# Four edits to a one-layer bidirectional mixer and expert kernel: scan order, values as one 512-column unit, fewer states, a stacked gate product

## The reference

```python
# mLSTM heads (keys and values of 128): states per chunk, both directions
c_new = a_old * c_st + a_new * (sum_l e_l v_l k_l^T)     # the same for the vector n
h = (S v + a * (q C_prev)) / max(|den|, exp(-m))
# gated linear attention heads (keys of 64, values of 128), per direction d
la = log_sigmoid(a_lr[:, 16 d:16 d + 16] @ w_a2[d] + b_a[d]) / 16      # low-rank gate, rank 16
S_t = diag(exp(la_t)) S_{t-1} + k_t v_t^T;   o_t = q_t S_t
```

## Time and profile before

| | |
|---|---|
| median of 3 runs | 1364.94 us (1364.13 to 1365.88) |
| profiled execution | 1364.38 us, span 1362.7 us |
| granted TensorE clock, mean | 0.978 |
| value stage | 196.5 to 257.5 us |
| first scan | 257.5 to 333.3 us |
| o0 to the end of the query unit | 333.3 to 445.4 us |
| second scan | 559.7 to 629.2 us |
| TensorE, VectorE, ScalarE, GpSimd busy | 94%, 70%, 57%, 9% of the span |

### The profile page before, as it was taken

One profiled execution on the slowest core, in us unless ns is written; L12 is line 12 of the kernel. 1 busy time (PEld: TensorE's weight loads), 2 busy tenths in 40 slices (PEclk: granted clock), 3 DMA queues, 4 the chain that ended last, 5 costly groups with the idle time before them and its releaser, 6 DMA issues.

```text
span 1362.7 us, 19538 instructions
## 1 busy us (share of the span) xinstructions
PE 1278.2 (94%) x7427; PEld 1119.3 (82%) x7427; DVE 953.1 (70%) x1114; ACT 773.2 (57%) x918; POOL 119.2 (9%) x127
## 2 busy tenths in 40 slices
PE   5899999899999999989999399999999999999994
PEld 4888799898987999867888388888888888888883
DVE  5757420278655772476545878888888888888887
ACT  6643320375213644574334257777777777777785
POOL 1100000010000000013000020111111111111034
PEclk9999979999999999999999699999999999999997
DMA  9851151143445321304213879999999999999995
GB/s 369 271 120 34 62 158 44 39 137 121 155 186 185 124 81 76 140 1 170 81 75 140 322 267 367 388 406 397 397 397 395 397 394 397 391 402 392 400 318 207
DMA packets 78686, 320.45 MB, mean 235 GB/s; under 512 B 5544, under 2 KB 32200, under 8 KB 48856
## 3 DMA queue, kind: packets, MB, share of 16 engines
q1 hardware_dynamic: 71360, 291.18, 54.4%
q0 software_dynamic: 7264, 28.40, 8.3%
HBM read 292.20 MB, written 35.75 MB: 241 GB/s over the span
## 4 chain that ended last, share of the span: by engine, by line
PE 80%; DVE 10%; ACT 5%; DMA 3%; issue 2%; SPq 0%; POOLq 0%; DVEq 0%; ACTq 0%
PE psum L2538 36%; PE psum L2192 7%; PE psum L2474 6%; PE psum L2250 5%; PE psum L2251 5%; PE psum L2252 5%; PE psum L2278 1%; DMA ada_raw<-w_ada_units 1%; PE psum L2286 1%; PE psum L2287 1%; PE psum L2266 1%; PE psum L2093 1%; PE psum L2561 1%; ACT g_ps L1124 1%; PE psum L2555 1%
## 5 line engine op out<-in xcount | busy, mean ns | idle before, releaser
L1955 DVE TENSOR_TENSOR e_lo<-e_raw,e_hi 128x2048 fp32r<-128x2048 f32 x192 | 432.8, 2287 | 43.1 <-ACT e_hi L1274 43.0
L1274 ACT ACTIVATE e_hi<-e_raw 128x2048 fp32r<-128x2048 f32 x192 | 365.9, 1916 | 83.3 <-PE psum L2538 82.1
L2538 PE MATMUL psum<-e_hi,xt_hi 128*128 128x512 f32 x496 | 153.3, 390 | 0.1
L2538 PE MATMUL psum<-e_lo,xt_hi 128*128 128x512 f32 x496 | 152.9, 389 | 0.0
L2538 PE MATMUL psum<-e_hi,xt_lo 128*128 128x512 f32 x496 | 152.8, 389 | 0.0
L2250 PE MATMUL psum<-w_hi,h_hi 128*128 128x256 f32 x512 | 147.1, 287 | 0.5 <-issue 0.5
L2251 PE MATMUL psum<-w_hi,h_lo 128*128 128x256 f32 x512 | 145.8, 285 | 0.0
L2252 PE MATMUL psum<-w_lo,h_hi 128*128 128x256 f32 x512 | 145.8, 285 | 0.0
L2538 PEld LDWEIGHTS psum<-e_hi,xt_lo 128*128 128x128 f32 x496 | 93.1, 188 | 19.6
L2538 PEld LDWEIGHTS psum<-e_lo,xt_hi 128*128 128x128 f32 x496 | 93.1, 188 | 19.5
L2538 PEld LDWEIGHTS psum<-e_hi,xt_hi 128*128 128x128 f32 x496 | 92.8, 188 | 19.8 <-DVE xt_lo L1959 0.5
(11 more groups left out here) (414 smaller groups left out, 2330.3 us busy)
## 6 DMA issues: line engine op xcount, KB each, us to landing
...
```

The costliest lines, as they stand in the source:

```text
L1274: act.activation(e_hi[u % EH][:], e_raw[u][:], ACT.Copy).then_inc(e_hi_ok, 1)
L1955: dve.tensor_tensor(e_lo[u][:], e_raw[u][:], e_hi[u % EH][:], ALU.subtract).then_inc(e_lo_ok, 1)
L2538: m = pe.matmul(o[:, BANK * b:BANK * (b + 1)], x[:, k, :], w[:, D * j + BANK * b:D * j + BANK * (b + 1)], start=a, stop=z)
```

## The change

Four edits at once.

1. **Values as one unit.** v1 is loaded into a buffer of its own right behind v0 and split right behind it; the two halves' `hi` and `lo` lie so that one access of 2 x 256 columns covers both. TensorE runs 10 tiles of 24 products of 512 columns, one bank each; each is evacuated by one instruction. Row loads for the context's third and fourth `bc` buffers wait for all ten tiles.
2. **First scan.** Steps 18 and 19 do no transposes, key scaling, state products or state update (N_STEPS = 18). split_lo(o0) moves in front of the wait for the last numerators.
3. **Gate product.** The 32 gate rows of a direction, their `hi` and their `lo` are stacked on 96 partitions (zx), the weights likewise (zw), so that one fp32r product of 96 rows gives the sum of three. ScalarE makes the `hi` parts between the sigmoids, VectorE the `lo` parts between columns 11 and 12.
4. **Second scan.** On ScalarE wo_hi_part goes in front of gla_carry; on VectorE wo_lo_part works on the part of the step before (steps 2 to 9); GpSimd's square waits until VectorE has made g_kx three steps on, its product until g_qz three steps on.

```diff
+        V1 = AT["in", "v1"]
+        v1_raw = at("v1_raw", AT_RING + 24 * KB, [P, KC, UW])
+        vv_hi = at("vv_hi", AT_RING + 16 * KB, [P, 4, KC, UW], F32R)[:, 0:4:3, :, :]
+        vv_lo = at("vv_lo", AT_RING + 8 * KB, [P, 3, KC, UW], F32R)[:, 0:3:2, :, :]
...
+        zx = [at(f"zx{d}", AT_OUT + (36 + 5 * d) * KB, [P, ALL], F32R) for d in range(2)]
+        zw = at("zw", AT_OUT + 46 * KB, [P, 2 * GK_W], F32R)
+        zw_hi = at("zw_hi", AT_OUT + 48 * KB, [P, 2 * GK_W], F32R)
...
+        N_STEPS = 2 * TA - 2
...
             def load_unit(n):
-                if n >= 10 and n - 2 != O0:
+                if n == V1:
+                    sp.wait_ge(raw_full[0], 48)
+                elif n >= 10 and n - 2 != O0:
                     wait_used(sp, n - 2)
-                sp.dma_start(raw[n % 2][:], unit_src(*STREAM[n])).then_inc(raw_full[n % 2], 16)
+                sp.dma_start(raw_of(n)[:], unit_src(*STREAM[n])).then_inc(raw_full[n % 2], 16)
...
             load_bc(1, *scan_chunk(1))
-            sp.wait_ge(tok_mm, 5)
+            sp.wait_ge(tok_mm, 10)
             load_bc(2, 0, 1)
-            sp.wait_ge(tok_mm, 10)
             load_bc(3, 1, 0)
...
             for l in range(TL, 2 * TL):
                 t = second_visit(l)
                 pool.wait_ge(og_done, l + 1)
+                pool.wait_ge(kx_ready, 16 + min(l + 4, 2 * TL))
                 if l >= TL + 2:
                     pool.wait_ge(sq_read, l - TL - 1)
                 pool.tensor_tensor(g_sq[l % 2][:], og(t), og(t), ALU.mult).then_inc(gla_sq, 1)
+                pool.wait_ge(gx_ready, min(l + 4, 2 * TL))
                 v = og(t).rearrange("p (u n) -> p u n", u=2)
                 pool.tensor_tensor(v, v, silu_r(t), ALU.mult).then_inc(fin_done, 1)
...
             conv_first(6, 0, 0, False)
             conv_first(7, 0, 1, False)
             split_hi(13)
+            split_hi(14)
             conv_silu(6, 0, 0)
             conv_silu(7, 0, 1)
             conv_first(8, 0, 2, False)
             conv_first(9, 0, 3, False)
-            split_hi(14)
             conv_silu(8, 0, 2)
             conv_silu(9, 0, 3)
             act.wait_ge(stat_ready, 1)
-            for u in range(2):
-                for j in range(5):
-                    p = 5 * u + j
-                    if p % 2 == 0:
-                        act.wait_ge(tok_mm, p + 1)
-                        for r in range(2):
-                            i = act.activation(v_ext[:, 2 * j + r, 2 * u:2 * u + 2, 0:HD], tokv(p, r), ACT.Copy)
-                        i.then_inc(tok_act, 1)
+            for p in range(0, TA, 2):
+                act.wait_ge(tok_mm, p + 1)
+                act.activation(v_ext[:, p, :, 0:HD], tokv(p), ACT.Copy).then_inc(tok_act, 1)
...
             def ml_front(t, l, d, c):
-                act.wait_ge(kt_mm, t + 1)
-                at_least(act, kv_mm, t - 1)
-                for h in range(NH):
-                    i = act.activation(ml_kh[d][:, h, :], kt_ps[d][:, h, :], ACT.Copy,
-                                       scale=cst[:, 1, ds(c, 1), NH * d + h])
-                i.then_inc(kh_ready, 1)
+                if t < N_STEPS:
+                    act.wait_ge(kt_mm, t + 1)
+                    at_least(act, kv_mm, t - 1)
+                    for h in range(NH):
+                        i = act.activation(ml_kh[d][:, h, :], kt_ps[d][:, h, :], ACT.Copy,
+                                           scale=cst[:, 1, ds(c, 1), NH * d + h])
+                    i.then_inc(kh_ready, 1)
...
             o_gates(0)
             split_hi(17)
+            for d in range(2):
+                q = slice(32 * d, 32 * (d + 1))
+                act.activation(zx[d][q, :], gate_rows[q, :], ACT.Copy)
+            act.activation(zw_hi[64:96, :], col("w_gla2")[64:96, :], ACT.Copy).then_inc(z_hi_ok, 1)
             o_gates(1)
+            for d in range(2):
+                q = slice(32 * d, 32 * (d + 1))
+                act.activation(zx[d][64:96, :], gate_rows[q, :], ACT.Copy)
+            act.activation(zw[0:64, :], col("w_gla2")[0:64, :], ACT.Copy).then_inc(z_hi_ok, 1)
...
                     gla_exps(l + 2)
+                if 1 <= l < 9:
+                    wo_hi_part(l - 1)
                 if 1 <= l <= N_STATE:
                     gla_carry(l - 1)
-                if 1 <= l < 9:
-                    wo_hi_part(l - 1)
...
             split_lo(13)
+            split_lo(14)
             conv_taps(8, 0, 2)
             conv_taps(9, 0, 3)
 
             dve.wait_ge(stat_mm, 1)
             dve.tensor_copy(cst[:].rearrange("p q c s -> p (q c s)"), psum[:, 7 * BANK:7 * BANK + 3 * TA * 2 * NH]).then_inc(stat_ready, 1)
-            split_lo(14)
             dve.memset(v_ext[:, :, :, HD:HD + 1], 1.0).then_inc(ones_set, 1)
-            for u in range(2):
-                for j in range(5):
-                    p = 5 * u + j
-                    if p % 2 == 1:
-                        dve.wait_ge(tok_mm, p + 1)
-                        for r in range(2):
-                            i = dve.tensor_copy(v_ext[:, 2 * j + r, 2 * u:2 * u + 2, 0:HD], tokv(p, r))
-                        i.then_inc(tok_dve, 1)
+            for p in range(1, TA, 2):
+                dve.wait_ge(tok_mm, p + 1)
+                dve.tensor_copy(v_ext[:, p, :, 0:HD], tokv(p)).then_inc(tok_dve, 1)
...
+            def ml_back(t, l, d, c):
+                if t < N_STEPS:
+                    ml_state(t, l, d)
                 if l is None:
                     return
+                if l == 2 * TL - 1:
+                    split_lo(O0)
                 dve.wait_ge(num_mm, l + 1)
...
             scan_steps(dve, ml_front, ml_back)
-            split_lo(O0)
...
-            ada_columns(10, 11, 12)
+            ada_columns(10, 11)
+            dve.wait_ge(z_hi_ok, Z_HI + 1)
+            for d in range(2):
+                q = slice(32 * d, 32 * (d + 1))
+                dve.tensor_tensor(zx[d][32 * (1 - d):32 * (2 - d), :], gate_rows[q, :], zx[d][q, :], ALU.subtract)
+            dve.tensor_tensor(zw[64:96, :], col("w_gla2")[64:96, :], zw_hi[64:96, :], ALU.subtract).then_inc(z_lo_ok, 1)
+            ada_columns(12)
...
                     gla_scores(l + 1)
-                if 1 <= l < 9:
-                    wo_lo_part(l - 1)
+                if 2 <= l < 10:
+                    wo_lo_part(l - 2)
...
-            tok_unit("v0", 13, h_hi, h_lo, 0)
-            tok_unit("v1", 14, h_hi, h_lo, 0)
+            unit_ready(V1)
+            for p in range(TA):
+                if p >= TOK_BANKS:
+                    pair_out(pe, p - TOK_BANKS)
+                o = psum[:, BANK * (p % TOK_BANKS):BANK * (p % TOK_BANKS + 1)]
+                c = slice(P * p, P * (p + 1))
+                for k in range(KC):
+                    pe.matmul(o, h_hi[:, k, c], vv_hi[:, :, k, :], start=k == 0, stop=False)
+                    pe.matmul(o, h_lo[:, k, c], vv_hi[:, :, k, :], start=False, stop=False)
+                    last = pe.matmul(o, h_hi[:, k, c], vv_lo[:, :, k, :], start=False, stop=k == KC - 1)
+                last.then_inc(tok_mm, 1)
...
+                if t >= N_STEPS:
+                    return
                 at_least(pe, kh_ready, t - 1)
...
-                pe.wait_ge(kh_ready, t + 1)
-                at_least(pe, c_done, t)
                 vc = lambda h: v_ext[:, ds(c, 1), h, :]
-                for h in range(NH):
-                    i = pe.matmul(kv_ps[:, h // 2, h % 2, :], ml_kh[d][:, h, :], vc(h), start=True, stop=True)
-                i.then_inc(kv_mm, 1)
+                if t < N_STEPS:
+                    pe.wait_ge(kh_ready, t + 1)
+                    at_least(pe, c_done, t)
+                    for h in range(NH):
+                        i = pe.matmul(kv_ps[:, h // 2, h % 2, :], ml_kh[d][:, h, :], vc(h), start=True, stop=True)
+                    i.then_inc(kv_mm, 1)
+                else:
+                    pe.wait_ge(c_done, t - 1)
...
+                if i == 0:
+                    pe.wait_ge(z_hi_ok, Z_HI + 2)
+                    pe.wait_ge(z_lo_ok, Z_LO + 1)
+                w = lambda dp: zw[0:96, P * dp:P * (dp + 1)]
                 if i < 8:
                     q = CTX + BANK * (i % 2)
-                    pe.matmul(z_ps(i), w(i // 2), gate_rows[:, q:q + BANK], start=True, stop=True).then_inc(z_mm, 1)
+                    pe.matmul(z_ps(i), w(i // 2), zx[i // 4][0:96, q:q + BANK], start=True, stop=True).then_inc(z_mm, 1)
                 else:
                     for j in range(2):
-                        x = pe.matmul(z_ps(i)[:, CTX * j:CTX * (j + 1)], w(2 * (i - 8) + j), gate_rows[:, 0:CTX], start=True, stop=True)
+                        x = pe.matmul(z_ps(i)[:, CTX * j:CTX * (j + 1)], w(2 * (i - 8) + j), zx[i - 8][0:96, 0:CTX], start=True, stop=True)
                     x.then_inc(z_mm, 1)
```

30 lines of the change are left out of this document (19 added, 11 removed).

## The result

| | before | changed |
|---|---|---|
| median of the first runs | 1364.54 us (1363.11 to 1365.88) | 1341.81 us (1341.10 to 1349.21) |
| all executions in this study | 40: median 1363.2, mean 1363.4, 1359.5 to 1369.7 | 14: median 1342.2, mean 1343.3, 1339.6 to 1349.2 |

The median of the first runs is that of four executions; a fifth of the changed kernel took 1343.04. The direction was right and the gain was forecast too small.

The account below looks back on a forecast made before the run. TensorE, busy 94% of the span, was taken as the bound. Terms 3.05 + 2.4 + 6.3 + 4.9 + 1.2 = 17.85 us off the profiled 1364.38 gave 1346.5, 1347.1 as median; range 1344.3 to 1351.5.

Parts of the forecast that it names:

- Values: Value stage: 240 products of 512 columns for 480 of 256 save 3.05 us; bounds 0 to 3.2.
- Rival E: Value products: pitch is columns plus a trifle, so the values give only 0.6 us; 1349.5 us, chance 0.04.
- Last states: End of first scan and o stage: 4.1 us less one half-clock spell of 1.7 gives 2.4; bounds 0.7 to 4.1.
- rival A: End of first scan: no spell of half clock in the new waits; 1345.4 us, chance 0.13.
- Gate product: Gate stage: one-pass pieces at 0.23 us instead of 0.86 save 6.3 us on TensorE; bounds 0 and 6.5.
- Second scan: First-half steps at 3.93 us instead of 4.59 save 4.9; g_kx without GpSimd beside it in the second half saves 1.2.
- C: Second scan keeps another loop, step near 4.35 us, first-half gain only 2; 1350.0 us, chance 0.13.
- D: Gate product saves only half, as TensorE meets late columns or evacuations; 1350.2 us, chance 0.08.
- G: Reordered scan keeps its waits and the gate stack stays multi-pass; 1359.5 us, chance 0.02.
- B: End of first scan: half-clock spells in both new waits; 1348.8 us, chance 0.13.
- part 4: Second scan, first half, eight steps with output-weight splits: gain 4.9 us; bounds 6.3 (TensorE alone) and 1.
- F: Slower: TensorE's clock stays low after the first scan's new waits, deciding from about 18 us at 1.2 GHz; chance 0.01.

Follow-up runs that it names:

- spread_filled: Changed kernel with the little gate-row products spread behind the last two query tiles' slices, plus unread products in TensorE's waits at the first scan's end and behind the query tile: 1338.49 us.
- quiet_undo_values: spread_filled with the values as two units of 256 columns again: 1341.11 us.
- first trace: The profiled execution of the unaltered changed kernel, slowest of its set: 1349.21 us, span 1347.5.
- undo_values: Changed kernel with the values as before, two units of 256 columns, second load behind the last query tile: 1348.21 us.
- undo_gate: Changed kernel with the gate product in fp32 over 128 rows, as before: 1350.01 us.
- undo_scan1: Changed kernel with all twenty states of the first scan and unit o0's split behind the last output, as before: 1347.81 us.
- quiet_undo_scan1: spread_filled with all twenty first-scan states and o0's split behind the last output, without the unread products in the first scan: 1342.16 us.
- third trace: Changed kernel run again without edit, traced once more: median 1341.92 us, span of the trace 1340.0.
- the second: Changed kernel run again without edit, for another trace: median 1344.91 us, span of the trace 1345.4.

## Why the forecast was right and where it failed

- **Values: right.** 3.05 forecast, 3.0 to 3.2 at equal spells, 3.24 with none. Start to start, the 240 products of 512 columns in spread_filled are 0.2267 us apart and the 480 of 256 in quiet_undo_values 0.1200: the pitches of the earlier trace rows held. Rival E, which gave 0.6, is out. (The Trainium skill's formula for a single product in TensorE: Matmul & The Clock Gate, section Back-to-back issue gap, would make the two cost nearly alike, an estimated 0.6 us apart; the stage windows differ by 3.24 us.) The second load and the zero fill cost nothing that shows.
- **Last states: the step that failed.** "This trace drops to half clock after idles of 1.05 and 0.79 close together ... So I charge one spell at half clock, 1.7 us, and take 2.4 us." The waits came as worked out, 1.39 and 1.92 us in the first trace, but a spell behind them came in only three of the nine traces that have this part and no filler there (330.0 in the first trace, and undo_values and undo_gate). Where it stays away and the old order has its own spell behind the wait for o_lo, the gain is the gross 4.1: 0.14 in the scan (74.57 us for undo_scan1's 74.71) and 3.9 in the o stage. So rival A, 1345.4, was the likeliest case and stood at 0.13. The 1.7 us that the sum credits for the old order's spell is not certain either: three of the four traces of that order have it, quiet_undo_scan1 has not, and there the gain is 2.39. That this is the forecast's 2.4 is luck, since it is another sum (neither spell, instead of both). Over the traces, 2.4 + 1.7 x (3/4 - 3/9) gives about 3.1 us as an estimate of the average gain.
- **The same mistake at a larger size.** The forecast also carried the other spells of its one trace over, as things the change leaves alone: "The first 22 or so products run at the half clock in any case", and the spell at the scan's start. In the third trace the half clock at the values' start lasts 6.8 us instead of 13.7, which is worth 3.3 us, and the one at the scan's start is absent, which is worth 1.0 (scan 75.74 us before, 74.71 in undo_scan1, which has the same twenty states and no spell there). I took one trace's falls of the clock for what the program does; they are what it does in some executions.
- **Gate product: right.** 6.3 forecast, 6.32 to 6.33 in each pair of traces; a piece takes 0.23 us, as its price of the earlier trace rows had it for 128 rows; nothing in the stage waits for a column or an evacuation.
- **Second scan: right.** 4.9 + 1.2 = 6.1 forecast, 6.1 to 6.4 measured to the end. The starts of the scores in the first half are 3.87 us apart (561.92 to 573.53, three steps) where 3.93 was forecast. GpSimd's waits give their 1.2 in the scan (1.3 measured) and 0.7 to 0.9 in all. The last wo_lo, which moved beside GpSimd's square, took 1.23 us for 0.74 in the trace. (The estimate of 1 us from the Trainium skill's SBUF — State Buffer, section SBUF: two separate sides, was twice too large for it; the square had begun 0.36 us before it, at 590.46, and took 1.04.)
- **Rivals.** C, D, E and G are out by the stages above; B, spells in both waits, is in no trace. The range's floor was said to be A with part 4 at its bound, which gives 1344.0 (1345.4 less 6.3 - 4.9), not 1344.3; the measured time lies below both. F asked for 18 us of extra work at 1.2 GHz; the longest new spells are 3.4 to 6.8 us, and no run of the changed kernel comes near the one before.

**The rest of the miss.** On the average, 40 executions of the kernel before have a mean of 1363.4 and 14 of the changed one 1343.3: 20.1 us, for the 17.85 of the sum. Of the 2.25 between them the estimate above explains 0.7 (3.1 for 2.4). The rest is not attributed; it is no larger than the differences between sets (the kernel before's medians lie between 1361.46 and 1364.54). The forecast time was higher by another 1.5 us because its base, a median of three at 1364.94, lay that far above the mean of the forty.

The median shown first, 1341.81, is lower still. Four of its five executions were probably of the kind of the third trace (execution 1341.75, clock 0.979 as theirs); that is inferred from their times and mean clocks alone, for those four have no trace. The third trace is 22.6 us shorter than the profiled one before, 4.8 more than the sum. By stages: 2.65 of that in the scan and the o stage (5.05 for 2.4: the spell charged and the one at the scan's start), 3.3 in the shorter spell at the values' start, and 1.2 lost again, because this trace reaches the little products later (186.51 for 185.32 us). Gate stage and second scan give 0.1.

**The wait at 142.** The first trace idles 3.9 us for a key tile, the second 1.7 and the third 1.1, and the traces show why. First and third:

```profile
87.92 1.92 ACT L871 ACTIVATE w_hi<-raw 128x2048 fp32r<-128x2048 f32 x1 [4.54 <-DMA raw<-w_in_units]
...
142.44 1.19 PE L2223 MATMUL psum<-h_hi,w_hi 128*128 128x512 f32 x2 [3.89 <-DVE kT L1536]
```
```profile
88.37 1.92 ACT L871 ACTIVATE w_hi<-raw 128x2048 fp32r<-128x2048 f32 x1 [1.73 <-DMA raw<-w_in_units]
...
142.91 0.70 PE L2223 MATMUL psum<-h_hi,w_hi 128*128 128x512 f32 x2 [1.10 <-DVE kT L1536]
```

ScalarE's split of that unit waits for its landing. From the split, ScalarE and VectorE take 54.5 us to the tile in every one of the eighteen traces, and TensorE takes 56.5 us from the stage's first product (82.02 and 85.27 us here) to the wait; the load is issued 1.6 us before that product. What is left to vary is the load's time from issue to landing: 7.5 us in the first trace (80.40 to 87.9), 5.3 in the second, 4.7 in the third (83.64 to 88.3), and less 3.6 these are the three waits. The third trace began the stage 3.3 us later than the first and reached the tile only 0.5 later. A spell at 141 to 144 us stands in seven of the eight traces with the longer of these waits (1.98 to 4.01 us; the eighth is the kernel before, 2.30) and in none of the ten others (1.08 to 1.78), and the three traces with a spell at 330 are among the seven.

**What stays open.** What makes the landing of that load take 4.7 us or 7.5; what decides whether the clock falls at a wait that some traces pass; and whether the changed kernel has a shorter spell at the values' start more often than the one before (13.7, 13.7 and 10.2 with two units; 6.8 to 13.7 with one), or whether the few traces only happened so. No run was made for any of these.
